# Raw rows into the first product, the token factor spread by TensorE, panels between the shifted copies, and layer norm sums added by VectorE first

## The reference, cut to what matters

```python
hn = rms_norm(x, cv_attn_norm_g)            # x * rsqrt(mean(x^2) + 1e-6) * g, per token
proj = hn @ w_in                            # 1024 -> 768 + 768 + 256
a    = proj[..., :768] + b_glu[:768]
gate = proj[..., 768:1536] + b_glu[768:]
u = a * sigmoid(gate)
c = depthwise_conv(u, 31 taps, causal) + dw_b
c = silu(layer_norm(c, ln_g, ln_b))         # mean and variance over the 768 channels
m = memory_attention(proj[..., 1536:], ...) # 4 heads of 64, keys and values from mem
h = x + concat([c, m]) @ w_out              # 1024 -> 1024
```

## Time and profile before

| | us |
|---|---|
| median of 3 runs | 2197.9 (2196.93 to 2197.91) |
| the profiled execution | 2198.4 |
| its span | 2196.6 |
| TensorE busy | 2159.6 (98%) |
| TensorE weight load busy | 1824.2 (83%) |
| VectorE busy | 1682.1 (77%) |
| ScalarE busy | 1406.0 (64%) |
| GpSimd busy | 69.8 (3%) |
| DMA, mean | 253 GB/s |

### The profile page before, as it was taken

One profiled execution on the slowest core, in us unless ns is written; L12 is line 12 of the kernel. 1 busy time (PEld: TensorE's weight loads), 2 busy tenths in 40 slices (PEclk: granted clock), 3 DMA queues, 4 the chain that ended last, 5 costly groups with the idle time before them and its releaser, 6 DMA issues.

```text
span 2196.6 us, 36183 instructions
## 1 busy us (share of the span) xinstructions
PE 2159.6 (98%) x11790; PEld 1824.2 (83%) x11790; DVE 1682.1 (77%) x2164; ACT 1406.0 (64%) x1877; POOL 69.8 (3%) x72
## 2 busy tenths in 40 slices
PE   8999999999999999999999999999999999999998
PEld 7789987778888888888888888787799888779987
DVE  5666658699999999999999999866576556657654
ACT  4454537578787878878887878745655434565543
POOL 0000004210000000000000000000010000001000
PEclk9999999999999999999999999999999999999999
DMA  8345563299999999999999999854445555444554
GB/s 276 119 169 183 165 202 124 102 345 344 362 373 360 371 354 357 382 351 350 363 374 353 375 348 368 312 167 145 149 164 181 195 186 185 147 151 164 178 196 143
DMA packets 153215, 556.42 MB, mean 253 GB/s; under 512 B 16976, under 2 KB 17104, under 8 KB 152912
## 3 DMA queue, kind: packets, MB, share of 16 engines
q1 hardware_dynamic: 152608, 553.17, 70.6%
q10 hardware_dynamic: 432, 1.03, 0.1%
HBM read 552.19 MB, written 1.93 MB: 252 GB/s over the span
## 4 chain that ended last, share of the span: by engine, by line
PE 87%; issue 7%; DVE 3%; ACT 1%; DMA 1%; POOL 0%; DVEq 0%; SPq 0%; ACTq 0%; POOLq 0%
PE L L2144 59%; PE L L2197 9%; PE L L2736 6%; PE L L2826 3%; PE TB L2212 2%; PE L L2161 2%; PE SC L2401 1%; DVE wlo L1246 1%; PE SC L2283 1%; PE TB L2302 1%; PE SC L2618 1%; PE L L2342 1%; PE SC L2626 1%; PE L L2456 1%; DMA raw<-w 0%
## 5 line engine op out<-in xcount | busy, mean ns | idle before, releaser
L1246 DVE TENSOR_TENSOR wlo<-deep,whi 128x1024 fp32r<-128x1024 f32 x682 | 810.0, 1223 | 43.2 <-ACT whi L700 12.6
L700 ACT ACTIVATE whi<-deep 128x1024 fp32r<-128x1024 f32 x682 | 713.2, 1060 | 132.8 <-PE L L2144 130.0
L1246 DVE TENSOR_TENSOR wlo<-raw,whi 128x1024 fp32r<-128x1024 f32 x353 | 427.2, 1225 | 264.7 <-ACT whi L700 260.2
L700 ACT ACTIVATE whi<-raw 128x1024 fp32r<-128x1024 f32 x353 | 367.6, 1057 | 310.0 <-PE L L2144 150.1
L2144 PE MATMUL L<-whi,xhi 128*128 128x512 f32 (+1 forms) x1136 | 447.9, 394 | 3.0 <-DVE wlo L1246 2.6
L2144 PE MATMUL L<-whi,xlo 128*128 128x512 f32 (+1 forms) x1136 | 442.1, 389 | 0.0
L2144 PE MATMUL L<-wlo,xhi 128*128 128x512 f32 (+1 forms) x1136 | 441.4, 389 | 0.0
L2144 PEld LDWEIGHTS L<-whi,xhi 128*128 128x128 f32 x1136 | 213.7, 188 | 49.1 <-DVE wlo L1246 6.7
L2144 PEld LDWEIGHTS L<-whi,xlo 128*128 128x128 f32 x1136 | 213.7, 188 | 45.0
L2144 PEld LDWEIGHTS L<-wlo,xhi 128*128 128x128 f32 x1136 | 213.8, 188 | 42.2
L2144 PE MATMUL L<-whi,mhi 128*128 128x512 f32 x448 | 175.1, 391 | 0.0
(11 more groups left out here) (382 smaller groups left out, 3196.9 us busy)
## 6 DMA issues: line engine op xcount, KB each, us to landing
deep<-wm SPq DMA_DIRECT2D x679, 512.0 KB, 5.5
raw<-wm SPq DMA_DIRECT2D x245, 512.0 KB, 3.4
raw<-w SPq DMA_DIRECT2D x112, 512.0 KB, 4.3
shifted<-gated SPq DMA_DIRECT2D x12, 286.0 KB, 5.1
mbuf<-mem SPq DMA_DIRECT2D x2, 1024.0 KB, 8.5
const<-const SPq DMA_DIRECT2D x1, 1312.0 KB, 7.3
out<-hn SPq DMA_DIRECT2D x2, 512.0 KB, 2.6
gated<-u SPq DMA_DIRECT2D x3, 288.0 KB, 2.6
```

The lines of the kernel that those rows point to most:

```text
L700: act(hi, slots[:, slot, :], ACT.Copy).then_inc(w.s.hi, 1)
L1246: v.tensor_tensor(lo, slots[:, slot, :], hi.bitcast(F32), ALU.subtract).then_inc(w.s.lo, 1)
```

## The change

It works on the first mixer, and the numbers and products stay the same.

1. Rows: `h` (raw x) is turned, not `hn`. Two groups are turned ahead of panel 0, one each ahead of panels 1 and 2. The factor 1/rms goes on a diagonal (VectorE), is spread by TensorE ahead of panel 2, copied to `rowx`, and multiplied into both banks of each gate chunk and into the memory query.
2. ScalarE's queue loads the constants before the second half of x; one filler matmul is left of three. VectorE's preparations move behind its four low parts, and its split of panel 3 behind them.
3. SP's list: panels 10 and 11 to 14 move between the waits for the gated output and the shifted copies; the masks are loaded after panel 25.
4. Layer norm: VectorE adds the three chunks (and their squares) first, TensorE sums two blocks instead of six.
5. Output panels: (0,0), (0,1), (0,2), transposes of the memory keys, (1,0), scores of pair 0, (1,1), scores of pair 1, transposes, (1,2), transposes, values, (0,3), (1,3), transposes of h. The weights are stored in that order.

```diff
@@ SyncE
             panels(A, lambda i: d["w1"][SLOTS + i], SLOTS, SLOTS)
-            e.dma_start(const[:, MASKS:NCO], d["const"][:, MASKS:NCO]).then_inc(s_masks, 16)
...
+            first = 26
+            up_to(8, 11)
+            gated_out(0)
+            up_to(11, 14)
+            shifted_in(0)
+            up_to(14, 15)
+            gated_out(1)
+            up_to(15, 18)
+            shifted_in(1)
+            up_to(18, 19)
+            gated_out(2)
+            shifted_in(2)
+            up_to(19, first)
+            e.dma_start(const[:, MASKS:NCO], d["const"][:, MASKS:NCO]).then_inc(s_masks, 16)
@@ ScalarE
+            e.dma_start(const[:, 0:MASKS], d["const"][:, 0:MASKS]).then_inc(s_in[0], 16)
             e.dma_start(h[:, 1, :], d["x"][P:S, :]).then_inc(s_x1, 16)
-            e.dma_start(const[:, 0:MASKS], d["const"][:, 0:MASKS]).then_inc(s_in[0], 16)
             e.dma_start(small[:, :], d["small"]).then_inc(s_in[1], 16)
...
-            split_to(w, 1)
-            e.wait_ge(w.s.nr, 1)
-            act(hn[:, 1, :], h[:, 1, :], ACT.Copy, scale=norm_cols(w, 1)[:, 1:2]).then_inc(s_xr, 1)
             e.wait_ge(s_in[1], 16)
             for q in range(4):
                 turned_group(w, q, lambda k: sp("cvn", k, 1))
-                if q < 2:
-                    split_to(w, q + 2)
+                if q < 3:
+                    split_to(w, q + 1)
...
-            silus(0)
-            silus(1)
+            for c in range(3):
+                silus(c)
             head_squares(w, ((s_ev, 5), [(mkv[:, :, 0:256], PT[:, 0, 1, :].rearrange("p (t n) -> p t n", t=T))]))
-            silus(2)
             split_to(w, w.n["p"] + 3)
             turned_heads(w, [(mkT, 2, sp("memk"))])
             split_to(w, w.n["p"] + 5)
 
             def between(s):
 
-                if s >= 0:
-                    split_to(w, w.n["p"] + min(s + 6, 8))
+                if s < 0:
+                    split_to(w, w.n["p"] + 6)
+                elif s == 1:
+                    split_to(w, w.n["p"] + 8)
@@ VectorE
+            for q in range(4):
+                turned_group(w, q, lambda k: sp("cvn", k, 1))
+                if q < 3:
+                    split_to(w, q + 1)
+                if q == 0:
+                    e.wait_ge(w.s.nr, 1)
+                    for t in range(T):
+                        i = v.tensor_scalar(sg[:, 1, t * P:(t + 1) * P], ident, norm_cols(w, 1)[:, t:t + 1], None, ALU.mult)
+                    i.then_inc(s_dg, 1)
             v.reduce_sum(same[:, :], ident.rearrange("p (j n) -> p n j", n=QC), axis=AX.X)
...
+            e.wait_ge(s_rall, 1)
+            w.link(v.tensor_copy(rowx[:, :], SC[0][:, 0:S]))
...
+                v.tensor_tensor(pair(sg[:, 0, :]), pair(banks[1][:, :]), per_token, ALU.mult).then_inc(s_gate, 1)
+                w.link(v.tensor_tensor(pair(sg[:, 1, :]), pair(banks[0][:, :]), per_token, ALU.mult))
+                e.sem_inc(A.free)
                 e.wait_ge(s_sig, c + 1)
...
+                    w.link(v.tensor_tensor(pair(sg[:, 1, :]), cacc[:, 0:2, :], cacc[:, 2:4, :], ALU.add))
             convolved(2)
+            v.tensor_tensor(pair(sg[:, 1, :]), pair(sg[:, 1, :]), cacc[:, 4:6, :], ALU.add).then_inc(s_ksum, 1)
...
+            e.wait_ge(s_lsq, 2)
+            w.link(v.tensor_tensor(u[:, 0:2, 0:S], u[:, 0:2, 0:S], u[:, 2:4, 0:S], ALU.add))
+            e.wait_ge(s_lsq, 3)
+            v.tensor_tensor(u[:, 0:2, 0:S], u[:, 0:2, 0:S], u[:, 4:6, 0:S], ALU.add).then_inc(s_qsum, 1)
             split_to(w, w.n["p"] + 6)
             e.wait_ge(s_lvar, 1)
...
             lows(2)
+            split_to(w, w.n["p"] + 3)
             head_scale(w, mkv[:, :, 0:256], 48, 4, 1)
-            split_to(w, w.n["p"] + 3)
             turned_heads(w, [(mkT, 2, sp("memk"))])
             split_to(w, w.n["p"] + 5)
             memory = [([plain], False, [BIG, BIG], False, 6 + i) for i in range(2)]
             attention(w, memory, SLOTS_MEM, scored=0)
+            split_to(w, w.n["p"] + 6)
             attention(w, memory, SLOTS_MEM, scored=1)
@@ TensorE
-            warm(3, SC[0])
+            warm(1, SC[0])
...
+            def first_rows(panel):
+
+                if panel in (1, 2):
+                    turn_group(w, h, panel + 1)
+                if panel == 2:
+                    spread_factors(SC[0], 1, (s_dg, 1))
+                e.wait_ge(w.s.tfree, w.at("t", 1 if panel < 3 else 2))
+            e.wait_ge(s_in[2], 16)
+            e.wait_ge(s_x1, 16)
+            for q in range(2):
+                turn_group(w, h, q)
+            chunk_features(w, before=first_rows)
...
-                    for k in range(FC):
-                        ins = mm(SC[1][:, 0:S], ones, cacc[:, k, :], start=(k == 0), stop=(k == FC - 1))
+                    e.wait_ge(s_ksum, 1)
+                    for f in range(2):
+                        ins = mm(SC[1][:, 0:S], ones, sg[:, 1, f * S:(f + 1) * S], start=(f == 0), stop=(f == 1))
...
             for j in range(3):
                 e.wait_ge(s_llo, j + 1)
                 out_panel(0, j)
-                if j == 1:
-                    e.wait_ge(A.zrdy, 2)
-                    turn(w, [(c * S + t * P, mkv[:, t, c * P:(c + 1) * P]) for c in range(2) for t in range(T)])
+            e.wait_ge(A.zrdy, 2)
+            turn(w, [(c * S + t * P, mkv[:, t, c * P:(c + 1) * P]) for c in range(2) for t in range(T)])
+            out_panel(1, 0)
             e.wait_ge(w.s.tfree, w.at("t", 2))
             e.wait_ge(s_lsc, 3)
             attention(w, memory, SLOTS_MEM, scored=0)
-            out_panel(1, 0)
+            out_panel(1, 1)
             attention(w, memory, SLOTS_MEM, scored=1)
             placed = attention(w, memory, SLOTS_MEM, lone_output, None, out_panels)
             placed(1)
             out_panel(0, 3)
-            out_panel(1, 2)
+            out_panel(1, 3)
             e.wait_ge(s_h, 1)
             for q in range(2):
                 turn_group(w, h, q)
-            out_panel(1, 3)
```

More of the change, by code:

```diff
@@ L300, in build @@
         s_ln = sem("s_ln")
-        s_xr = sem("s_xr")
+        s_gate = sem("s_gate")
+        s_ksum = sem("s_ksum")
+        s_qsum = sem("s_qsum")
         s_x1 = sem("s_x1")
@@ L497, in _, with gated_out, shifted_in @@
             panels(A, lambda i: d["w1"][SLOTS + i], SLOTS, SLOTS)
-            e.dma_start(const[:, MASKS:NCO], d["const"][:, MASKS:NCO]).then_inc(s_masks, 16)
-            first = 26
-            for c, (begin, end) in enumerate(((2 * SLOTS, 10), (10, 14), (14, 18))):
-                panels(A, lambda i: d["w1"][begin + i], end - begin, begin)
+            def gated_out(c):
                 e.wait_ge(s_ev, c + 1)
                 e.dma_start(d["gated"][c], u[:, 2 * c:2 * c + 2, :].rearrange("p f n -> p (f n)")).then_inc(s_gated, 16)
+            def shifted_in(c):
                 e.wait_ge(s_gated, 16 * (c + 1))
@@ L508, in _, with up_to @@
                                 ).then_inc(s_shift[c], 16)
-            panels(A, lambda i: d["w1"][18 + i], first - 18, 18)
+            def up_to(begin, end):
+                panels(A, lambda i: d["w1"][begin + i], end - begin, begin)
+            first = 26
[12 more added lines that the diff above has]
+            e.dma_start(const[:, MASKS:NCO], d["const"][:, MASKS:NCO]).then_inc(s_masks, 16)
             e.wait_ge(A.tdone, 8)
@@ L1510, in _ @@
             v.tensor_tensor(rr[:, :, 1, :], router, rr[:, :, 0, :].bitcast(F32), ALU.subtract).then_inc(s_pre, 1)
[L1511 to L1514, removed]
+            e.wait_ge(s_rall, 1)
+            w.link(v.tensor_copy(rowx[:, :], SC[0][:, 0:S]))
+            pair = lambda x: x.rearrange("p (a s) -> p a s", s=S)
             def glu(c, banks):
+                per_token = rowx[:, :].unsqueeze(1).to_broadcast([P, 2, S])
+                v.tensor_tensor(pair(sg[:, 0, :]), pair(banks[1][:, :]), per_token, ALU.mult).then_inc(s_gate, 1)
+                w.link(v.tensor_tensor(pair(sg[:, 1, :]), pair(banks[0][:, :]), per_token, ALU.mult))
+                e.sem_inc(A.free)
                 e.wait_ge(s_sig, c + 1)
                 for f in range(2):
-                    i = v.scalar_tensor_tensor(u[:, 2 * c + f, PAD:PAD + S], banks[0][:, f * S:(f + 1) * S],
+                    i = v.scalar_tensor_tensor(u[:, 2 * c + f, PAD:PAD + S], sg[:, 1, f * S:(f + 1) * S],
                                                sp("bglu", 2 * c + f, 1), sg[:, 0, f * S:(f + 1) * S], ALU.add, ALU.mult)
                 w.link(i)
-                e.sem_inc(A.free)
                 e.sem_inc(s_ev)
@@ L1554, in _ @@
             for t in range(T):
-                w.link(v.tensor_copy(z[:, t, 0:256], banks[t][:, 0:256]))
+                w.link(v.tensor_scalar(z[:, t, 0:256], banks[t][:, 0:256], norm_cols(w, 2)[:, t:t + 1], None, ALU.mult))
             e.sem_inc(A.free)
@@ L1615, in _ @@
             split_to(w, w.n["p"] + 2)
-            w.n["p"] -= 2
-            add_rows(w, settled(w, 2), 1, s_h)
+            w.n["p"] -= 1
```

(22 more changed lines are left out.)

43 lines of the change are left out of this document (18 added, 25 removed).

## The result

The changed kernel takes 2205.7 us (median of 7 runs, 2203.6 to 2209.6); the kernel before took 2197.3 (2196.6 to 2200.2) on the same chip. The ratio is 1.0036, 95% interval [1.0027, 1.0045]: slower by 0.36%, about 7.9 us. The forecast was 2201.7 with a range to 2206.0. Its direction was right and its size half of what came. The time lies inside the range by 0.3, and above both values of rival 2 (clock pays at every hole; 3.8 + 1.7 and one more stretch at the start give 2203.4 and 2205.1). As a shift it is +7.9 by the ratio and +8.4 by the medians, against +8.1 for the end of the range, so that it fell inside is near to luck.

A forecast was written before the change was run, and what follows sets the result against it. TensorE, busy 2159.6 of 2196.6 us, was taken as the bound. Terms 1.4 - 3.9 + 4.6 + 1.7 = +3.8 us on a median of 2197.9 gave 2201.7, with a range from 2194.8 to 2206.0.

The forecast's parts named there:

- rival 2: Clock pays at every hole, also behind panel 21's: +5.5, or +7.2 with a second stretch at the start; 2204 us; 34%.
- A: Start to the end of the first convolution's input: +2.35 less 0.9 for the late split, +1.4 us (bounds -1.0 and +3.1).
- B: Layer norm: fewer TensorE passes and no half-clock stretch, less new waits, -3.9 us (bounds -2.2 and -5.2).
- C: Output panels and attention: waits from the new order and one more panel before attention's end, +4.6 us (bounds +2.5, +5.5).
- D: Clock behind the new holes of the output stage: one half-clock stretch, behind the longer hole, +1.7 us (bounds 0, +3.4).
- first panel at 12.8: Start: the first panel begins at 12.8 us, 1.2 earlier than the 14.04 before.
- one half-clock stretch, 1.7: Start: after about 3.2 us of nothing the first panel meets the low clock, cost 1.7 us (bounds 0 and 3.4).
- wait before panel 3, 1.2: Start: TensorE waits 1.2 us before the fourth panel, whose split stands behind other work on VectorE; panel at 25.75.
- late split before panel 11: First convolutions: the reordered loads take away the wait on a late split, 0.9 us.
- later stages pass the shift on unchanged: After the changed stretch: same code, TensorE bound, so the shift of +3.8 us arrives at the end.
- hole of 2.7 at panel 21: Output panel (1,0): TensorE stands 2.7 us, its split being behind the copy of the memory keys' transposes.
- 3.5 idle before the feed-forward stage: End of the output stage: no panel covers the chain of high and low parts, so TensorE idles 3.5 us of 4.56.

The follow-up runs named there:

- experiment 2: The changed kernel with part 5 undone (old order of output panels, attention and splits): 2197.2 us, ratio 0.9996 to the kernel before.
- experiment 3: The kernel before with part 4 alone (the layer norm sums): 2193.8 us, ratio 0.9978.
- experiment 4: The kernel before with parts 3 and 4 (new order of loads and layer norm sums): 2191.7 us, ratio 0.9971.
- experiment 8: Experiment 4 with two filler matmuls in place of three and VectorE scaling its rows ahead of panel 0's split: 2191.3 us, ratio 0.9971.
- experiment 1: The changed kernel with panel 21's split on ScalarE and VectorE ahead of their copy of the memory keys' transposes: 2200.2 us, ratio 1.0011.
- experiment 5: Experiment 2 with three filler matmuls between the first two groups' transposes and panel 0: 2194.2 us, ratio 0.9981.
- experiment 7: Experiment 1 with the transposes of two groups of h ahead of output panel (1,3): 2197.2 us, ratio 0.9999.
- experiment 9: Experiment 2 with fillers before panel 0 and VectorE's split of panel 3 ahead of its preparations: 2193.1 us, ratio 0.9972.

## Why the prediction came out as it did

By the ratios, the change falls into four steps: parts 1 and 2 +5.5, part 3 -1.5, part 4 -4.8, part 5 +8.8. They are differences along one series of kernels, so that they add up to the measured 7.9 (8.0 by rounding) is arithmetic and confirms nothing; what they show is the size of each. Predicted: A (parts 1 to 3) +1.4, B (part 4) -3.9, C and D (part 5) +6.3; together +3.8.

- **A, first panel at 12.8:** it started at 13.29. The small table landed 8.44 after its issue instead of 8.0, which is nearly all of the 0.5.
- **A, one half-clock stretch, 1.7:** right in kind and too small. The first panel took 4.81, or 1.9 more than the second one's 2.88; in experiment 2 it took 5.46, all of it at half clock, 2.6 more.
- **A, wait before panel 3, 1.2:** it was 1.13, at 26.30 (predicted 25.75). The late split before panel 11 went, as predicted.
- **A, total +1.4:** +2.0 in the changed kernel's profile, +4.0 by the ratios of experiments 2 and 3. Two steps failed. The clock's share was taken too small (1.7 for 1.9 to 2.9, with the transposes behind the panel). And the sentence that later stages pass the shift on unchanged was wrong: experiments 2 and 4 are 4.1 apart at the first convolution and 6.1 at the end, with equal code between. 1.4 of these 2.0 are four waits of TensorE, at about 270, 705, 1195 and 1415 us, of which these lines show the first and the last, in experiment 4 and then in experiment 2:

```profile
269.04 0.47 PE L2174 MATMUL L<-whi,fhi 128*128 128x512 f32 x1 [1.36 <-DVE wlo L1267]
1411.63 0.66 PE L2242 MATMUL TB<-const,mbuf 128*128 128x128 f32 x4 [1.62 <-DVE x2lo L1314]
```
```profile
273.50 0.47 PE L2175 MATMUL L<-whi,fhi 128*128 128x512 f32 x1 [1.72 <-DVE wlo L1263]
1417.29 0.66 PE L2243 MATMUL TB<-const,mbuf 128*128 128x128 f32 x4 [2.13 <-DVE x2lo L1310]
```

  The four together are 3.8 us in every profile without parts 1 and 2 (before, experiments 3, 4 and 8) and 5.2 in every profile with them. Why they grow is open, and so are the other 0.6 us.
- **B, -3.9:** first output panel at X + 15.4, to the tenth. The new wait before the squares was 0.73 (predicted 0.8); no half-clock stretch. That the stretch of the earlier trace rows at 126 would go too when part 4 stands alone was not foreseen: -4.8 instead of -3.9.
- **C, hole of 2.7 at panel 21:** 2.77. **3.5 idle before the feed-forward stage:** 3.53, with 11.75 from panel (0,3) to the feed-forward stage, as before. From 96.79 to 129.12 it is 32.33, before 26.29: 6.04 more. Of that, 1.85 is the half clock at 108.88 (experiment 1), which leaves 4.2 for the order of the work, against 4.6 predicted.
- **D, one stretch, 1.7:** this is the term that was mis-sized. Both holes paid: 1.85 behind the one at panel 21 and 2.36 (5.46 less 3.10) behind the longer, plus 0.3 in the transposes after it; together 4.5 in place of 1.7. I had taken the clock once because no hole of this length was in the trace, and gave rival 2 almost the same chance; its condition, that the 2.7 us at panel 21 are real, came true. (Its two sums are 5.5 and 7.2, whose middle is 6.35 and not 6.1.)
- **The profile as a whole:** against the kernel before it is +2.0 (start) - 3.9 (layer norm) + 6.0 (panels and the clock at panel 21) + 2.7 (clock at the feed-forward stage) = +6.8. The later waits add 1.4. The spans differ by 10.0 (2206.6 and 2196.6), and the 1.8 that is left has the size of the one further half-clock stretch of this profile, at 385.71. The runs' ratio is smaller, 7.9, because the profiled execution is the longest.
- **Part 5's 8.8 has another base:** experiment 2, whose last two output panels run at full clock (5.75). The kernel before and the changed one both pay 1.6 there. In the profiles part 5 is 4.2 + 1.85 + 1.6 by the feed-forward stage and 2.7 behind it, 10.3; by the ratios 8.8.

The Trainium skill (TensorE: Matmul & The Clock Gate, "Why this matters for your kernels") says that idle gaps between bursts of matmuls bring the low clock back, and it says so of gaps longer than the 2.77 us at panel 21; the prediction read it as a rule for both holes, which is more than it states. The trace agrees with it for the hole of 3.53 us.

Where the page stops, the measurement decides: the hole of 2.77 us paid as well. Experiments 1, 5 and 7 show the price by taking a hole away or filling it.

## What to carry to other kernels

In a kernel bound by TensorE a wait can cost more than its length, by the low clock behind it: taking away one of 2.8 us gave 5.5 (2.8 and 1.85 of it seen at the place, most of the rest in a stretch whose tie to it is not shown), and the hole of 3.0 us before panel 0 cost up to 2.6 more in the panel behind it. The waits of 1.5 and 0.8 us in experiment 7 had no such price. When a step is moved on the engine that sets the end, move the other engines' lists with it: one `split_to` line in each of two lists decided 5.5 us. And if a hole can't be avoided, useless matmuls in it may help: before the first panel they gave 3.3 us back.

## What the runs showed of the hardware

- The granted clock of the profile shows 1.00 from the start in every kernel, while in the changed kernel and in experiment 2 the 256-column matmuls of the first panel begin 0.21 us apart and later 0.12 (4.81 and 5.46 us per panel against 2.88). At the start only the speed of the instructions tells the clock.
- The same code is at half clock in one execution and not in another. The transposes at 385.71 of the changed kernel and at 378.51 of the kernel before have the same waits ahead of them (1.48 and 0.16 us):

```profile
384.07 0.63 PE L2550 MATMUL TB<-const,z 128*128 128x128 f32 x4 [1.48 <-DVE PT L1412]
385.71 1.45 PE L2335 MATMUL TB<-const,hn 128*128 128x128 f32 x6 [0.16 <-ACT stat L822]
```
```profile
376.87 0.63 PE L2506 MATMUL TB<-const,z 128*128 128x128 f32 x4 [1.48 <-DVE PT L1394]
378.51 0.85 PE L2302 MATMUL TB<-const,hn 128*128 128x128 f32 x6 [0.16 <-ACT stat L799]
```

- The spans of the kernel before on one chip went from 2193.6 to 2199.6 us, with mean granted clocks from 0.999 down to 0.997. Experiments 4 and 9, without long holes, stay within 1.4 and 2.6 us; but experiment 3, also without, goes over 4.4, and experiment 2, with the hole before panel 0, over 3.0. That fewer holes make a kernel steadier is not shown.
